# Placing the weights of the seven-product pairs 32 bytes short of the streamed operand, modulo 512

## What is computed

```
def swiglu(h, w_gu, w_down):
    a, b = jnp.split(h @ w_gu, 2, axis=-1)
    return (jax.nn.silu(a) * b) @ w_down

# first block
    hn = rmsnorm(h, g_ffn[l])
    h = h + (jax.nn.silu(hn @ w_gate[l]) * (hn @ w_up[l])) @ w_down[l]
# second block, twice (ffn1, ffn2)
    h = modulate(rms_norm(x, g_ffn1[l]), sh1, sc1)
    x = x + 0.5 * gt1[:, None, :] * swiglu(h, w1_gu[l], w1_down[l])
```

## Time and profile before

| | us |
|---|---|
| runs, median of 3 | 2007.42 (2004.12 to 2008.17) |
| profiled execution, span from first to last instruction | 2004.3 |
| PE busy | 1982.4 (99%) |
| DVE busy | 1236.5 (62%) |
| POOL busy | 905.8 (45%) |
| ACT busy | 898.6 (45%) |

### The profile page before, as it was taken

One profiled execution on the slowest core, in us unless ns is written; L12 is line 12 of the kernel. 1 busy time (PEld: TensorE's weight loads), 2 busy tenths in 40 slices (PEclk: granted clock), 3 DMA queues, 4 the chain that ended last, 5 costly groups with the idle time before them and its releaser, 6 DMA issues.

```text
span 2004.3 us, 32457 instructions
## 1 busy us (share of the span) xinstructions
PE 1982.4 (99%) x11622; PEld 1717.1 (86%) x11622; DVE 1236.5 (62%) x1937; ACT 898.6 (45%) x1605; POOL 905.8 (45%) x458
## 2 busy tenths in 40 slices
PE   9999999999999999999999999999999999999998
PEld 7788788878999988899998888887777888999887
DVE  4675885346788787877768774463552247777111
ACT  4334444344566522556652252225663245666322
POOL 3344323326577655544445434443224445444443
PEclk9999999999999999999999999999999999999999
DMA  6243212212333286333338635322222223333321
GB/s 209 90 152 106 74 64 83 86 33 94 106 105 105 95 314 247 101 115 105 105 95 326 237 120 149 116 95 85 68 70 85 89 89 95 105 105 105 103 98 63
DMA packets 67246, 234.71 MB, mean 117 GB/s; under 512 B 7632, under 2 KB 9040, under 8 KB 66640
## 3 DMA queue, kind: packets, MB, share of 16 engines
q1 hardware_dynamic: 66432, 232.29, 35.3%
q10 hardware_dynamic: 720, 1.15, 0.2%
HBM read 225.54 MB, written 2.10 MB: 114 GB/s over the span
## 4 chain that ended last, share of the span: by engine, by line
PE 94%; DVE 3%; ACT 1%; issue 1%; DMA 0%; POOL 0%; SPq 0%; POOLq 0%; DVEq 0%; ACTq 0%
PE bank L2254 12%; PE bank L2255 12%; PE bank L2260 12%; PE bank L2433 9%; PE bank L2434 9%; PE bank L2437 9%; PE bank L2378 5%; PE bank L2379 5%; PE bank L2384 5%; PE bank L2228 1%; PE bank L2230 1%; PE bank L2229 1%; PE bank L2552 1%; PE bank L2560 1%; PE bank L2553 1%; PE bank L2870 1%
## 5 line engine op out<-in xcount | busy, mean ns | idle before, releaser
L538 POOL TENSOR_TENSOR wlo<-raw,whi 128x1024 fp32r<-128x1024 f32 x233 | 579.9, 2490 | 807.7 <-ACT whi L657 807.4
L657 ACT ACTIVATE whi<-raw 128x1024 fp32r<-128x1024 f32 x233 | 245.8, 1057 | 475.0 <-PE bank L2384 217.7
L2254 PE MATMUL bank<-xh,whi 128*128 128x512 f32 x764 | 302.0, 395 | 1.2 <-DVE xl L1355 0.9
L2255 PE MATMUL bank<-xl,whi 128*128 128x512 f32 x764 | 297.7, 390 | 0.0
L2378 PE MATMUL bank<-hh,whi 128*128 (+1 forms) x480 | 186.9, 389 | 1.0 <-ACT whi L657 1.0
L2379 PE MATMUL bank<-hl,whi 128*128 (+1 forms) x480 | 186.8, 389 | 0.0
L2260 PE MATMUL bank<-xh,wlo 128*128 128x512 f32 x736 | 181.6, 389 | 0.0
L2254 PEld LDWEIGHTS bank<-xh,whi 128*128 128x128 f32 x764 | 143.5, 188 | 34.9 <-issue 4.7
L2255 PEld LDWEIGHTS bank<-xl,whi 128*128 128x128 f32 x764 | 143.5, 188 | 29.5 <-issue 0.7
L2260 PEld LDWEIGHTS bank<-xh,wlo 128*128 128x128 f32 x736 | 138.1, 188 | 28.9
L2434 PE MATMUL bank<-xl,whi 128*128 128x256 f32 x648 | 162.5, 283 | 0.0
(11 more groups left out here) (396 smaller groups left out, 4510.0 us busy)
## 6 DMA issues: line engine op xcount, KB each, us to landing
raw<-units SPq DMA_DIRECT2D x341, 512.0 KB, 3.7
ada_w<-ada_rows SPq DMA_DIRECT2D x72, 512.0 KB, 5.6
h<-x_t SPq DMA_DIRECT2D x8, 256.0 KB, 5.3
out_t<-h SPq DMA_DIRECT2D x8, 256.0 KB, 2.1
raw<-units SPq DMA_DIRECT2D x4, 256.0 KB, 4.5
mem_in<-mem_t SPq DMA_DIRECT2D x1, 1024.0 KB, 11.2
turned_q<-proj SPq DMA_DIRECT2D x4, 256.0 KB, 5.1
dec<-decays SPq DMA_DIRECT2D x4, 256.0 KB, 4.7
```

Of the source, the lines that this page charges most:

```text
L538: pool.tensor_tensor(wlo[:, j % 2 * UNIT:(j % 2 + 1) * UNIT], raw[:, j * UNIT:(j + 1) * UNIT], whi[:, j % 2 * UNIT:(j % 2 + 1) * UNIT].bit ...
L657: act.activation(whi[:, v % 2 * UNIT:(v % 2 + 1) * UNIT], raw[:, slot * UNIT:(slot + 1) * UNIT], ACT.Copy).then_inc(hi_ready, 1)
L2254: mm(bank[:, 0:n], wh, chunk(rhs[0], t, n), start=t == 0, stop=False)
L2255: mm(bank[:, 0:n], wh, chunk(rhs[1], t, n), start=False, stop=False)
```

## The change

The weights of the seven-product pairs get places that are 32 bytes below the place of the streamed operands modulo 512. For this the small buffers `es`, `gmod`, `mx`, `nm`, `sm` and `rs` move between the large ones, `whi` and `wlo` get 512 bytes behind them, and paddings keep the large buffers at equal places. `whi` and `wlo` themselves stay at equal places for all other layers; the pairs address them through `PAIR_HI` and `PAIR_LO`, of which the up half begins 32 bytes ahead of the slot and the gate half 480 bytes behind it. `w_t1`, `w_t2` and `w_t3_high` move by 480 bytes, and padding brings `w_t3_low` to the same place. Which instructions run, in what order and with which waits, stays as it was.

```diff
+LINE = 128
...
-        raw, whi, wlo = sb("raw", 4 * UNIT), sb("whi", 2 * UNIT, f32r), sb("wlo", 2 * UNIT, f32r)
+        raw = sb("raw", 4 * UNIT)
+        es, gmod = sb("es", 64), sb("gmod", 6 * C + 1)
+        sb("ahead_of_whi", 8)
+        whi_at = nc.sbuf_base
+        whi = sb("whi", 2 * UNIT, f32r)
+        sb("behind_whi", LINE)
+        wlo_at = nc.sbuf_base
+        wlo = sb("wlo", 2 * UNIT, f32r)
+        sb("behind_wlo", LINE)
...
-        ssum, rstd = sb("ssum", T), sb("rstd", T)
+        ssum = sb("ssum", T)
+        mx, nm = sb("mx", 64), sb("nm", 64)
+        rstd = sb("rstd", T)
...
+        sm, rs = sb("sm", 64), sb("rs", 64)
...
-        side_at = arena_at - 12 * 1024
+        side_at = arena_at - 4 * LINE - 12 * 1024
...
-        mx, nm, sm, rs, es = (sb(n, 64) for n in ("mx", "nm", "sm", "rs", "es"))
...
-        gmod = sb("gmod", 6 * C + 1)
...
+        sb("ahead_of_w_t3_low", (x_at // 32 - 1 - (nc.sbuf_base + 31) // 32) % 16 * 8)
         w_t3_low = sb("w_t3_low", 4 * P, f32r)
...
-        w_t1 = at("w_t1", 8, 8 * P, f32r, base=side_at)
-        w_t2 = at("w_t2", 0, 8 * P, f32r, base=xn_at)
-        w_t3_high = at("w_t3_high", 4, 4 * P, f32r, base=xn_at)
+        short = 4 * LINE - 32
+        w_t1 = at("w_t1", 8, 8 * P, f32r, base=side_at + short)
+        w_t2 = at("w_t2", 0, 8 * P, f32r, base=xn_at + short)
+        w_t3_high = at("w_t3_high", 4, 4 * P, f32r, base=xn_at + short)
+        PAIR_HI = (at("up_hi", 0, UNIT, f32r, base=whi_at - 32), at("gate_hi", 4, UNIT, f32r, base=whi_at + short))
+        PAIR_LO = (at("up_lo", 0, UNIT, f32r, base=wlo_at - 32), at("gate_lo", 4, UNIT, f32r, base=wlo_at + short))
...
+        def pair_half(slots, slot, half):
+            return slots[slot][:, half * 4 * P:(half + 1) * 4 * P]
```

More of the change, by code:

```diff
@@ L356, in two_block_kernel @@
         GATE, UP = 1, 0
-        T_HI = {1: w_t1[:, 0:4 * P], 2: w_t2[:, 0:4 * P], 3: w_t3_high[:, :], 4: unit_half(whi, UP, 0)}
-        T_LO = {1: w_t1[:, 4 * P:8 * P], 2: w_t2[:, 4 * P:8 * P], 3: w_t3_low[:, :], 4: unit_half(wlo, UP, 0)}
+        T_HI = {1: w_t1[:, 0:4 * P], 2: w_t2[:, 0:4 * P], 3: w_t3_high[:, :], 4: pair_half(PAIR_HI, UP, 0)}
+        T_LO = {1: w_t1[:, 4 * P:8 * P], 2: w_t2[:, 4 * P:8 * P], 3: w_t3_low[:, :], 4: pair_half(PAIR_LO, UP, 0)}
         T_PLACE = {2: 1, 1: 2, 3: 3, 4: 4}
@@ L568, in gate_first @@
                     slot = (u1 + 2 * r) % 4
-                    pool.tensor_tensor(unit_half(wlo, GATE, 0), unit_half(raw, slot, 0), unit_half(whi, GATE, 0).bitcast(f32),
+                    pool.tensor_tensor(pair_half(PAIR_LO, GATE, 0), unit_half(raw, slot, 0), pair_half(PAIR_HI, GATE, 0).bitcast(f32),
                                        ALU.subtract).then_inc(first_lo, 1)
@@ L574, in gate_second @@
                     slot = (u1 + 2 * r) % 4
-                    pool.tensor_tensor(unit_half(wlo, GATE, 1), unit_half(raw, slot, 1), unit_half(whi, GATE, 1).bitcast(f32),
+                    pool.tensor_tensor(pair_half(PAIR_LO, GATE, 1), unit_half(raw, slot, 1), pair_half(PAIR_HI, GATE, 1).bitcast(f32),
                                        ALU.subtract).then_inc(lo_ready, 1)
@@ L580, in up_second @@
                     slot = (u1 + 2 * r + 1) % 4
-                    pool.tensor_tensor(unit_half(wlo, UP, 1), unit_half(raw, slot, 1), unit_half(whi, UP, 1).bitcast(f32),
+                    pool.tensor_tensor(pair_half(PAIR_LO, UP, 1), unit_half(raw, slot, 1), pair_half(PAIR_HI, UP, 1).bitcast(f32),
                                        ALU.subtract).then_inc(lo_ready, 1)
@@ L852, in gate_first @@
                     slot = raw_in(i, r, 0)
-                    act.activation(unit_half(whi, GATE, 0), unit_half(raw, slot, 0), ACT.Copy).then_inc(first_hi, 1)
+                    act.activation(pair_half(PAIR_HI, GATE, 0), unit_half(raw, slot, 0), ACT.Copy).then_inc(first_hi, 1)
                 def gate_second(i, g, r):
                     slot = raw_in(i, r, 0)
-                    act.activation(unit_half(whi, GATE, 1), unit_half(raw, slot, 1), ACT.Copy).then_inc(hi_ready, 1)
+                    act.activation(pair_half(PAIR_HI, GATE, 1), unit_half(raw, slot, 1), ACT.Copy).then_inc(hi_ready, 1)
                 def up_second(i, g, r):
                     slot = raw_in(i, r, 1)
-                    act.activation(unit_half(whi, UP, 1), unit_half(raw, slot, 1), ACT.Copy).then_inc(hi_ready, 1)
+                    act.activation(pair_half(PAIR_HI, UP, 1), unit_half(raw, slot, 1), ACT.Copy).then_inc(hi_ready, 1)
                 def part_out(r, dst):
@@ L2449, in gate_first @@
                     n = HN_BEFORE + G * k + g + 1
-                    product(left(banks[GATE_BANK[r]]), unit_half(whi, GATE, 0), unit_half(wlo, GATE, 0), x11,
+                    product(left(banks[GATE_BANK[r]]), pair_half(PAIR_HI, GATE, 0), pair_half(PAIR_LO, GATE, 0), x11,
                             (first_hi, n), (first_lo, n), True).then_inc(five_done, 1)
@@ L2457, in finish @@
                     pe.wait_ge(up_right, GN_BEFORE + G * k + g + 1)
-                    product(left(banks[UP_BANK]), unit_half(whi, UP, 1), unit_half(wlo, UP, 1), s4,
+                    product(left(banks[UP_BANK]), pair_half(PAIR_HI, UP, 1), pair_half(PAIR_LO, UP, 1), s4,
                             (hi_ready, u1 + 2 * g + 2), (lo_ready, u1 + 2 * g + 2), False).then_inc(unit_used, 1)
@@ L2461, in left_product @@
                     n = u1 + 2 * g + 1
-                    product(left(banks[LEFT_BANK]), unit_half(whi, GATE, 1), unit_half(wlo, GATE, 1), x12,
+                    product(left(banks[LEFT_BANK]), pair_half(PAIR_HI, GATE, 1), pair_half(PAIR_LO, GATE, 1), x12,
                             (hi_ready, n), (lo_ready, n), True).then_inc(unit_used, 1)
```

## The result

The changed kernel takes 1994.08 us (1993.54 to 1995.96, 5 runs) against 2006.21 us (2003.72 to 2008.17, 5 runs) of the kernel before: a ratio of 0.9946, with a 95% interval of 0.9935 to 0.9956. It is faster by 12.1 us, just under half of the 24.5 us of the forecast, and it lands on the time of the rival "half freed", 1994.

The account below looks back on a forecast made before the run. PE's issue rate was taken to bound the kernel: 27.2 us from faster pairs, less 0.6 for `w_t3_low` and 2.1 for `gu`, gave 24.5; 2004.3 - 24.5 + 3.1 = 1982.9 us, range 1975 to 2010.

Parts of the forecast that it names:

- half freed: Pairs: 32 short does what 160 short does, one meeting of load and stream remains; 117 ns, 13.0 us gained, 1994; chance 0.27.
- What bounds the kernel, and where the gain lies: PE's issue rate, busy 99%; only the three stretches of seven-product pairs change, at 120 ns per matmul.
- The floor of 113 ns: Streaming alone needs 113 ns per 256 columns, from 226 ns in the 512-column down layers; pairs lose 7 ns per matmul.
- The pace at 32 short: Pairs go from 120 to 114 ns per matmul, 6 ns on 4,536 matmuls, 27.2 us.
- the 160-short sample: `w_t3_low` before the change, 352 bytes from the streamed operands modulo 512; its loads and matmuls were 3 ns shorter.
- the account of load and stream meeting within 512 bytes: Pairs: equal places meet at the load's start and end; 32 short only once, 7 ns before the end.
- `w_t3_low`, 0.6 us: Deduction in the pairs for what this weight already has: 216 matmuls x 3 ns.
- What is late next: First stretch `gu`: DVE and ACT wait for each other, up to 4.3 us lost; half, 2.1 us, taken off.
- Writers: ACT, DVE and POOL writing weights 32 bytes aside in the pairs: a few ns, hidden; 8 us at most without cover.
- No effect: Pairs: `w_t3_low` gains by neighbours in the order, or the meeting shifts without shortening; 2008; chance 0.11.
- Slower: Pairs: the meeting moves to the load's end, where the next matmul waits; 20 us lost, 2028; chance 0.14.
- What would show it: Pairs' loads at 186 to 189 ns, matmuls 276 to 279, stretches 172 to 175 us; 512-column layers stay at 226 ns.

Follow-up runs that it names:

- the sizes: Kernel of matmuls alone, 128 to 512 columns streamed at several weight places; at equal places 111.7 ns up to 240 columns, 120.0 at 256, 226.7 at 512.
- lone matmuls: Small kernels running only blocks of matmuls, no other engine of the core at work, weight place varied; 256 columns took 119.9 ns at equal places, 116.75 at 32 short.
- all sixteen entries: Kernel of matmuls alone, the block at 8 behind entered sixteen times, after three matmuls of 300 to 360 columns; 115.6 ns each time.

## Why the first stretch gave less

The table by stage had put the danger in `gu`, and it was there; but the circle that binds is another one. VectorE's waits for the transfer between 540 and 680 us, in after and with the weights 8 behind:

```profile
DVE bank L1613 <- DMA raw<-units: 5.2, 14, 0.6
```

```profile
DVE bank L1616 <- DMA raw<-units: 0.4, 1, 0.4
```

The columns are us in total, times, longest. In after VectorE waits in every pair for the weights' transfer; before, none of its waits named a transfer. One round of it, from the timeline of after:

```profile
588.63 1.62 DVE L1613 TENSOR_TENSOR bank<-raw 128x512 f32<-128x512 f32 x1 [0.52 <-DMA raw<-units]
...
592.14 0.61 ACT L878 ACTIVATE up_hi<-raw 128x512 fp32r<-128x512 f32 x1
...
592.30 0.41 DVE L1640 TENSOR_TENSOR tmp<-bank,tmp 128x256 f32<-128x256 f32 x1
...
592.83 1.77 POOL L598 TENSOR_TENSOR up_lo<-raw,up_hi 128x512 fp32r<-128x512 f32 x1 [3.13 <-ACT up_hi L878]
...
592.87 0.35 PE L2450 MATMUL bank<-s,w_t 128*128 128x256 f32 x1
...
598.40 1.82 DVE L1613 TENSOR_TENSOR bank<-raw 128x512 f32<-128x512 f32 x1 [0.32 <-DMA raw<-units]
```

Two more sums and one step for the activations follow VectorE's first sum on its queue; ScalarE waits for that step, then makes the high part of the second up block; from it GpSimd makes the low part, which frees the raw slot at 594.60; the next unit lands 3.8 us later, and VectorE's next first sum starts at 598.40, at once. Over the stretch one such round takes 9.91 us on average (9.60 to 10.20; the one shown 9.77), and a pair at 116.7 ns only 84 x 116.7 = 9.80. So VectorE falls behind, its L1640 ends at 592.71, and PE, which wants the bank that it reads, starts L2450 just after. The pauses themselves cost 1.2 us more than those of the other stretches, (2.95 - 1.51) - (1.10 - 0.83); the rhythm that each pause breaks costs 0.48 ns on some 1,490 matmuls, 0.7 us. Together 1.9 us.

With the weights 8 behind a pair is 84 x 115.6 = 9.71 us, shorter still, and VectorE waits for the transfer once. There GpSimd's low part is shorter too; its rows in the same 140 us, after and 52 behind:

```profile
L598 POOL TENSOR_TENSOR up_lo<-raw,up_hi 128x512 fp32r<-128x512 f32 x14 | 24.6, 1760 | 41.5 <-ACT up_hi L878 41.5
```

```profile
L601 POOL TENSOR_TENSOR up_lo<-raw,up_hi 128x512 fp32r<-128x512 f32 x15 | 23.3, 1555 | 39.2 <-ACT up_hi L881 39.2
```

1.76 us against 1.55 (also 1.55 at 8 behind; 1.75 at 160 and at 76, 1.77 before). It frees the slot 0.2 us earlier. VectorE's first two sums of a pair read `raw` alone, and the one of them that runs beside a GpSimd subtraction is long, 1.6 to 1.8 us in after (the first sum above) where the other takes 0.7 or 0.8. With 8 behind it is shorter too:

```profile
596.02 1.59 DVE L1617 TENSOR_TENSOR bank<-raw 128x512 f32<-128x512 f32 x1
```

That is another 0.2 us off the round. Together they make up the 5.2/14 = 0.37 us of the wait. At 76, with the long low part and a pair that would take 9.52 us at 113.3 ns, VectorE does wait for the transfer, 2.4 us in 140. That this is why 8 behind has no such wait in most pairs is argued from the rows; no run changed GpSimd's place alone.

## Why the prediction was wrong, point by point

- **What bounds the kernel, and where the gain lies: right.** All of the change is in the three stretches, by pace; the 512-column layers stayed at 226 ns; nothing else moved.
- **The floor of 113 ns: right as a number.** 52 and 76 behind run at 113.3 ns in two stretches of the kernel. It was found by halving the 512-column pace; the sizes show that this holds only for the best place, since at equal places 32 cycles come on top of 256 columns as of 512.
- **The pace at 32 short: the step that failed.** "I take 114 ns, a gain of 6, nearest to the 512-column row, because of the two meetings the one at the start ... is the one that the 160-short sample lacks too." The gain is 119.83 - 116.70 = 3.13 ns where the waits are few; the mean of before holds what `w_t3_low` had already. 4,536 x 3.13 = 14.2 us; the pauses grew by 0.3 us in each stretch, 0.8 in all, and `gu` lost 1.9 more: 11.5, as measured. The choice rested on the account of load and stream meeting within 512 bytes. The runs speak against it at three points: the period is 256 bytes, 160 behind has no equal start and gains nothing, and shorter loads do not lower the cost in order of their length (at 512 columns they raise it). The sample nearest to the change, `w_t3_low` at 3 to 4 ns gain, was the row to trust: 352 and 480 differ by only 0.7 ns.
- **`w_t3_low`, 0.6 us: right** in size. The run of four that was shown took 0.46 us, 115 ns each; over all its 216 matmuls the mean before was 116.7, and lone matmuls at its place take 117.3.
- **What is late next: right in size by luck, not in kind.** 2.1 us were set aside for `gu`, half of a bound of 4.3, and 1.9 were lost. But they were expected of VectorE and ScalarE waiting for each other, with a PE that gains twice as much; they come by the raw slot and the transfer, 0.7 of them by the rhythm that the pauses break, and at 115.6 ns they are gone.
- **Writers: right for after.** The writes of weights took as long as before to 6 ns, or less, so nothing had to be hidden. At other distances GpSimd's time does follow the place, by 0.2 us per block, and VectorE's sum beside it.
- **The rivals.** "Half freed" had the time, 1994, by the right price: 32 short does what 160 short does, to 0.7 ns. Its reason, one meeting that remains, is not borne out. "No effect" was the case of two read ports that never wait, as the Trainium skill has it (SBUF — State Buffer, "Who interferes with whom"); lone matmuls that differ from 113 to 122 ns by the relative place alone show that for `f32r` the place matters, by whatever mechanism. "Slower" did not come.
- **What would show it.** The loads read 187 to 189 as asked, and the forecast still failed: at 160 behind they read 188 and 189 at a pace of 120.0. Nor did another engine take over, as short loads with long stretches were to mean: in the second and third stretch PE's pauses grew by 0.3 us of 177. The sign to ask for was the start-to-start time.

What stays open is the mechanism: why places 256 bytes apart are alike, why one place has several rhythms, and why bfloat16 shows no such cost. No run settles that.

## What to carry to other kernels

When one unit is busy 99% of the time, measure its own pace by start-to-start times and test a suspected address effect with lone instructions over all places, before a model of it is built from one sample; the lone pace carried over to the kernel to 0.1 ns in the settled part of every stretch that had few pauses. Look at what happens after a pause too: 52 behind has the best pace and was the fastest in each of its five runs (1977.4 to 1984.7 us), yet it fell into 118 to 120 ns in the first stretch; 76 did so too and came out no faster (1987.17) than 8 behind (1986.54), which held 115.6 in all sixteen entries and all stretches. And a faster engine tightens every circle that frees its buffers, so follow the circle (slot, transfer, writer), not only the engine that is busiest.

## What the runs showed of the hardware

- `f32r` matmuls of 256 columns take 113.3 to 122.2 ns according to the place of the weight relative to the stream modulo 256 bytes; 512 columns take 226.7 to 237.3. bfloat16 at 256 columns takes 109.2 ns at the four places tried, and `f32r` stands at 111.7 at 128 to 224 columns at the three places tried (240: 111.7 to 112.8).
- The same block, its weight 52 bytes behind, ran at 113.3 or 120.0 ns from one entry to the next and kept that rhythm to its end; in a kernel it was 113.3 up to a pause of 25 ns and 120.0 from there to the end of the stretch.
- One GpSimd subtraction of 512 columns took 1.55 us with its weight places 8 or 52 behind and 1.75 to 1.77 at 0, 160, 76 and 32 short.
